# Three weight buffers in place of two for the expert stage, and gate and up rows in runs of 2 KB

## The chip, the cores and the metric

The kernel runs on one core of one Trainium2 chip. Its engines are PE (the matmul engine, TensorE), DVE (VectorE), ACT (ScalarE), POOL (GpSimd) and SP (SyncE, which here only issues DMAs). The metric is the time of one execution on the device, in microseconds (us); lower is better. Everything computed is float32, or float32 split into a high and a low part.

## The reference

Two layers of a decoder trunk are computed for 512 tokens of width 1024. Only the second half of a layer is touched by the change:

```python
def hierarchical_moe(xn, w_rg, b_rg, w_re, b_re, w_g, w_u, w_d):
    t = xn.reshape(-1, d)
    ...                                   # top group of 4, then top 2 of its 4 experts
    gates = jnp.sum(jax.nn.one_hot(gid, N_EXPERTS) * w_e[..., None], axis=1)
    y = jnp.zeros_like(t)
    for e in range(N_EXPERTS):            # 16 experts
        hid = jax.nn.silu(t @ w_g[e]) * (t @ w_u[e])   # 1024 -> 256, twice
        y = y + gates[:, e:e + 1] * (hid @ w_d[e])     # 256 -> 1024
    return y

for l in range(DEPTH):                    # 2 layers
    ...                                   # three kinds of attention, gates, w_out
    x = x + jnp.sum(gates * proj, axis=2) @ w_out[l]
    x = x + hierarchical_moe(rms_norm(x, norm_ffn[l]), ...)
```

The weights of one expert are three matrices of 1 MiB each: gate and up of 1024x256, down of 256x1024.

## The kernel before

Each layer first runs a long chain of projections and attention, in which PE is fed by pieces of `w_in`, `w_branch` and `w_out` (256 KB each, tile `raw`). The last group is `w_out`. As its tiles are finished, DVE adds them to `x_rows` (the residual), POOL multiplies the sum by the gain of the norm into `rows` (`grow_rows`, 8 instructions of 128x512 for each layer, before `row_scale(1)` for all but the last), and SP stores `rows` to `xn_dram` in four DMAs of 512 KB (L1455, semaphore `xn_out`).

Then the router chooses experts: PE turns the left and right halves of `x_rows`, multiplies by the router's weights, and a chain of short DVE instructions (`route`, L1157 on) makes the table of rows for each expert. It waits for `row_scale(1)` by `scale_ready`. The last of the chain is `tab_i` (L1221, semaphore `r_addr`); while it runs, PE repeats dummy transposes (`keep_warm`, L595).

The expert stage takes the 16 experts in a fixed order (`ORDER`), one after the other, each with at most 128 tokens. For one expert e:

- POOL gathers its rows from `xn_dram` into `xg` (L836, two buffers), PE transposes them (`turn_chunk`, 8 transposes, L702), ACT and DVE split them into a high and a low part (`rows_hi`, `rows_lo`).
- The weights come in six pairs of 128x1024: roles 0 to 3 are gate and up (each pair holds two of the 8 blocks of 128 input rows), roles 4 and 5 are down. For each pair ACT writes the high part (`pair_hi`, L665) and DVE the low part (`pair_lo`, L671) into a ring of five places (`xT` and one in `wh`/`wl`). PE multiplies each split pair in three passes (`passes`, L599 to L601), so 24 matmuls for gate and up, and 12 for down.
- ACT and DVE form the hidden rows, PE turns them, and ACT copies the two halves of the result out of PSUM with the gate (L1018, L1024). POOL scatters them with an addition into the output (L842).

PE computes gate and up of expert e+1 while it is at step e, then down of e. ACT's instructions stand in program order: the copy L1018 of one half of the result, then `pair_hi` of the next pair, and so on.

The raw weights land in two buffers, each of six pairs: buffer 0 in `bqkv`, buffer 1 in `q_c` (gate and up) and `head_odd` (down). Expert e uses buffer e mod 2. SP issues all these DMAs. Experts 0 and 1 are loaded behind the last pieces of `w_out` (L1447). Then SP stores `rows`, loads the next layer's first pieces, and enters `experts_sp` (L847). Its step 1 waits for the first gather to land (`xg_in[0]`), and then issues gate and up of expert 2, each pair once DVE has read that place for expert 0; then it stores `x_rows` to the output; and then for each step gate and up of e+1 and down of e, each behind a wait for `pair_lo_ready`. One gate or up DMA (`load_gate_up`, L675) moves 256 KB. In memory a row of these matrices has 256 floats, so the block of rows `(k p)` gives each partition two runs of 1 KB. A down DMA moves 512 KB in runs of 2 KB.

At the end of layer 0 the last scatter must land, and then `x_rows` is read back from the output. `rows` and `x_rows` are not used between the store of `x_rows` and the next layer.

## Time and profile before

| | us |
|---|---|
| median of 3 runs | 1498.8 |
| lowest and highest run | 1497.61 and 1499.75 |
| the profiled execution's own time | 1496.16 |
| its span, from first to last instruction | 1494.3 |
| PE busy | 1442.4 |
| DVE busy | 893.3 |
| ACT busy | 854.4 |
| POOL busy | 405.1 |

The span is what the trace covers; the 1.86 us between it and the execution's own time lie outside it. Times in the rows are us from the start of the span, unless ns is written. A busy time of PE holds overlapped matmuls, so what counts for PE is the distance between starts. In rows of stretches a DMA share of 1.00 says that the core's 16 DMA engines were busy all the time. The expert stages run from about 580 to 745 us (layer 0) and from about 1322 us to the end (layer 1).

### The profile page before, as it was taken

To read this page: it belongs to the slowest core of one execution; us is meant where nothing else is said; L and a number is where in the kernel's file an instruction comes from. 1 tells how busy PE (TensorE), PEld (TensorE's weight loads), DVE (VectorE), ACT (ScalarE), POOL (GpSimd) and SP (SyncE) were. 2 spreads that over 40 slices of the span, in tenths; PEclk is the share of its full clock that TensorE was granted. 3 is DMA by queue.
4 is the path that set the end of the run, shared out by engine and by line. 5 is a ranking of instruction groups with operands and counts; after the bars stand their busy time and mean duration, and the time that the engine had idled before them with its cause. 6 is when DMAs were issued, how large, how long until landed. Compare 5 with 4: busy or idle time off the path is not lost.

```text
span 1494.3 us, 22177 instructions
## 1 busy us (share of the span) xinstructions
PE 1442.4 (97%) x7844; PEld 1142.2 (76%) x7844; DVE 893.3 (60%) x1742; ACT 854.4 (57%) x1588; POOL 405.1 (27%) x547
## 2 busy tenths in 40 slices
PE   8999999999999999999899999999999999999996
PEld 7787777777777887777677877777777788877775
DVE  4456655634554447989735566556345544489986
ACT  5456546655443335888734565466554434368886
POOL 5314227620000024242215043285200000242421
PEclk9999999999999999999999999999999999999998
DMA  7622222222233368999965222222222323769996
GB/s 196 135 66 69 58 71 64 58 64 64 64 98 97 114 213 272 355 348 350 248 151 121 72 64 64 62 64 60 64 64 64 120 85 111 248 241 348 347 354 196
DMA packets 156054, 220.55 MB, mean 148 GB/s; under 512 B 24851, under 2 KB 94163, under 8 KB 155940
## 3 DMA queue, kind: packets, MB, share of 16 engines
q1 hardware_dynamic: 143604, 194.82, 41.4%
q0 software_dynamic: 11328, 21.60, 7.0%
q10 hardware_dynamic: 1008, 2.69, 0.5%
q8 instruction: 63, 1.03, 0.3%
q14 instruction: 51, 0.42, 0.1%
HBM read 210.51 MB, written 25.49 MB: 158 GB/s over the span
## 4 chain that ended last, share of the span: by engine, by line
PE 81%; DVE 7%; ACT 5%; issue 3%; DMA 3%; POOL 0%; DVEq 0%; POOLq 0%; ACTq 0%; SPq 0%
PE bank L599 21%; PE bank L601 20%; PE bank L600 20%; PE bank L1650 4%; PE bank L1634 3%; PE bank L1623 3%; PE bank L1625 2%; DMA raw<-in_w_in_dram 2%; PE bank L702 2%; DVE xT L671 2%; ACT xT L665 1%; PE bank L1683 1%; PE bank L1686 1%; DVE wl L529 1%; DVE prob L2011 1%
## 5 line engine op out<-in xcount | busy, mean ns | idle before, releaser
L599 PE MATMUL bank<-wh,xT 128*128 128x512 f32 (+1 forms) x960 | 392.8, 409 | 9.1 <-DVE wl L529 5.9
L601 PE MATMUL bank<-wh,xT 128*128 128x512 f32 (+1 forms) x960 | 373.2, 389 | 0.0
L600 PE MATMUL bank<-wl,xT 128*128 128x512 f32 (+1 forms) x960 | 372.5, 388 | 0.0
L522 ACT ACTIVATE wh<-raw,gcol 128x512 fp32r<-128x512 f32 (+1 forms) x208 | 148.5, 715 | 250.7 <-PE bank L601 229.8
L529 DVE SCALAR_TENSOR_TENSOR wl<-raw,gcol,wh 128x512 fp32r<-128x512 f32 (+1 forms) x208 | 161.4, 780 | 156.4 <-ACT wh L522 151.6
L599 PEld LDWEIGHTS bank<-wh,xT 128*128 128x128 f32 x960 | 180.4, 188 | 67.8 <-issue 21.1
L601 PEld LDWEIGHTS bank<-wh,xT 128*128 128x128 f32 x960 | 180.2, 188 | 36.9
L600 PEld LDWEIGHTS bank<-wl,xT 128*128 128x128 f32 x960 | 180.8, 188 | 32.1 <-issue 1.4
L1801 ACT ACTIVATE prob<-prob,nmax 128x128 f32<-128x128 f32 (+2 forms) x192 | 106.7, 557 | 99.8 <-DVE nmax L2011 99.3
L2335 POOL TENSOR_TENSOR rows<-x_rows,ac 128x512 f32<-128x512 f32 x16 | 22.2, 1402 | 477.0 <-DVE x_rows L2078 477.0
L2011 DVE CUSTOM_DVE_ANT_0 prob<-bank,mask 128x128 f32<-128x128 f32 (+3 forms) x128 | 57.4, 487 | 138.8 <-PE bank L1625 78.1
L529 DVE SCALAR_TENSOR_TENSOR wl<-raw,wh 128x512 fp32r<-128x512 f32 (+1 forms) x92 | 64.2, 701 | 102.9 <-ACT wh L522 100.0
L522 ACT ACTIVATE wh<-raw 128x512 fp32r<-128x512 f32 (+1 forms) x92 | 57.2, 621 | 109.4 <-PE bank L601 109.3
L599 PE MATMUL bank<-wh,oT 128*128 128x512 f32 (+1 forms) x276 | 112.2, 406 | 3.7 <-issue 1.7
L601 PE MATMUL bank<-wh,oT 128*128 128x512 f32 (+1 forms) x276 | 106.3, 385 | 0.0
L600 PE MATMUL bank<-wl,oT 128*128 128x512 f32 (+1 forms) x276 | 106.0, 384 | 0.0
L671 DVE TENSOR_TENSOR xT<-bqkv,xT 128x1024 fp32r<-128x1024 f32 x76 | 91.2, 1219 | 10.6 <-ACT xT L665 10.3
L599 PE MATMUL bank<-xT,oT 128*128 128x512 f32 x204 | 85.5, 419 | 6.0 <-DVE xT L671 4.4
L842 POOL DMA_INDIRECT out_dram<-ac,tab_i x32 | 53.1, 1658 | 109.9 <-ACT ac L1024 96.5
L665 ACT ACTIVATE xT<-bqkv 128x1024 fp32r<-128x1024 f32 x76 | 78.7, 1057 | 2.9 <-DMA bqkv<-in_w_expert_down_dram 2.1
L601 PE MATMUL bank<-xT,oT 128*128 128x512 f32 x204 | 80.3, 393 | 0.0
L600 PE MATMUL bank<-xT,oT 128*128 128x512 f32 x204 | 79.9, 392 | 0.0
(321 smaller groups left out, 2668.4 us busy)
## 6 DMA issues: line engine op xcount, KB each, us to landing
raw<-in_w_in_dram SPq DMA_DIRECT2D x190, 256.0 KB, 2.7
bqkv<-in_w_expert_gate_dram SPq DMA_DIRECT2D x64, 256.0 KB
bqkv<-in_w_expert_up_dram SPq DMA_DIRECT2D x64, 256.0 KB
bqkv<-in_w_expert_down_dram SPq DMA_DIRECT2D x32, 512.0 KB
q_c<-in_w_expert_gate_dram SPq DMA_DIRECT2D x64, 256.0 KB
q_c<-in_w_expert_up_dram SPq DMA_DIRECT2D x64, 256.0 KB
head_odd<-in_w_expert_down_dram SPq DMA_DIRECT2D x32, 512.0 KB
raw<-in_w_branch_dram SPq DMA_DIRECT2D x48, 256.0 KB, 2.6
```

The source lines that it names most:

```text
L522: nc.scalar.activation(wh[:, i % HL, 0:width], raw[:, i % RAW, 0:width], ACT.Copy, scale=piece_gain(i))\
L529: nc.vector.scalar_tensor_tensor(out=wl[:, i % HL, 0:width], in0=raw[:, i % RAW, 0:width], scalar=piece_gain(i), in1=wh[:, i % HL, 0:width ...
L599: nc.tensor.matmul(out, lhs[0], rhs[0], start=start, stop=False)
L600: nc.tensor.matmul(out, lhs[0], rhs[1], start=False, stop=False)
L601: return nc.tensor.matmul(out, lhs[1], rhs[0], start=False, stop=stop)
L665: nc.scalar.activation(pair_half(pair_ring(e, j, par), 0), pair, ACT.Copy).then_inc(pair_hi_ready, 1)
L671: nc.vector.tensor_tensor(pair_half(pair_ring(e, j, par), 1), pair, pair_half(pair_ring(e, j, par), 0).bitcast(F32), ALU.subtract).then_in ...
L842: nc.gpsimd.indirect_dma_start(out=out_rows, out_offset=bass.IndirectOffsetOnAxis(ap=index, axis=0), in_=src, in_offset=None, bounds_check ...
L1623: mm = pe.matmul(out, q[r, c, qs], k[r, c, 0:w], start=(b == 0), stop=(b == 0 or col + w == 512))
L1650: mm = pe.matmul(o_bank[h * HD:(h + 1) * HD, block * P:(block + 1) * P], val[:, kt, vc:vc + HD], probT[:, h, col + kt * P:col + (kt + 1) * P],
L1801: act.activation(prob[:, h, col:col + w], prob[:, h, col:col + w], ACT.Exp, scale=-1.0, bias=nmax[:, m:m + 1], accum_out=den[:, m:m + 1]). ...
L2011: nc.vector.tensor_tensor_reduce(prob[:, h, col:col + w], sc_bank[h][:, col:col + w], add, -SOFT[b], 3.0e38, ALU.add, ALU.min, nmax[:, m:m ...
```

## The change

A third buffer is added (`NB = 3`), so that expert e uses buffer e mod 3. The new one has gate and up in `rows` and down in `x_rows`. Since `rows` is free once it has been stored to `xn_dram`, and `x_rows` once it has been stored to the output, SP's list at the start of the expert stage is written anew: wait for `xn_out`, issue gate and up of expert 2 with no further wait, wait for the first gather, store `x_rows`, issue gate and up of expert 3, wait for `x_stored`, issue down of expert 2. From then on gate and up of x+1 are issued ahead of down of x, for x from 3 on.

Second, gate and up are read as `(p k)` in place of `(k p)`: partition p takes the 8 rows 8p to 8p+7, which lie side by side, so that two of them are one run of 2 KB, and the next partition's run starts 8 KB further on. For the product to stay the same, the columns of the normed rows are permuted in the same way: `grow_rows` on POOL now reads its inputs in order and writes each group of 8 elements with a step of 128 elements (512 bytes). And in a pair the two gate blocks now stand ahead of the two up blocks, so that PE's moving operand of 512 columns is two runs of 256 with 256 others between them.

```diff
--- before.py
+++ after.py
@@ -39,6 +39,7 @@
 NCH = 23
 OVER_PLACED, OVER_LISTED, OVER_SLOTS = 37, 43, 4
 RAW, HL = 4, 3
+NB = 3
 BIAS_LEN = SEQ + P
 
 
@@ -310,8 +311,10 @@
         raw_slots = [bqkv.rearrange("p (j k c) -> p j k c", j=6, k=2),
                      q_c.rearrange("p h s -> p (h s)").rearrange("p (j k c) -> p j k c", j=4, k=2),
                      head_odd.rearrange("p (j k) c -> p j k c", j=2)]
+        third = [rows.rearrange("p j (k c) -> p j k c", k=2), x_rows.rearrange("p j (k c) -> p j k c", k=2)]
         pair_raw = [[raw_slots[0][:, j] for j in range(6)],
-                    [raw_slots[1][:, j] for j in range(4)] + [raw_slots[2][:, j] for j in range(2)]]
+                    [raw_slots[1][:, j] for j in range(4)] + [raw_slots[2][:, j] for j in range(2)],
+                    [third[0][:, j] for j in range(4)] + [third[1][:, j] for j in range(2)]]
         pair_w = xT.rearrange("p a k s -> p (a k s)").rearrange("p (r h k c) -> p r h k c", r=4, h=2, k=2)
         xgT_all = oT0.rearrange("p a k s -> p (a k s)").rearrange("p (b h k s) -> p b h k s", b=2, h=2, k=KD)
         xgT = [xgT_all[:, 0], xgT_all[:, 1]]
...
@@ -636,9 +640,8 @@
         def pair_place(e, j, par, half):
 
             role = pair_role(e, j)
-            if role < 4:
-                return pair_raw[1 - par][role], pair_in[1 - par][role], 32 * (half + par + 1)
-            return pair_raw[par][role], pair_in[par][role], 16 * (half + 1)
+            x = e + 1 if role < 4 else e
+            return pair_raw[x % NB][role], pair_in[x % NB][role], (32 if role < 4 else 16) * (x // NB + 1)
 
         def pair_multiplied(eng, e, j):
 
@@ -675,18 +678,25 @@
         def load_gate_up(sp, expert, j, par, s_):
 
             for half, w in ((0, "w_expert_gate"), (1, "w_expert_up")):
-                src = at(t[w].rearrange("l e (k p) f -> (l e) p k f", p=P), expert)
-                sp.dma_start(pair_raw[par][j][:, :, half * FF:(half + 1) * FF], src[:, 2 * j:2 * j + 2, :]).then_inc(s_, 16)
+                src = at(t[w].rearrange("l e (p k) f -> (l e) p (k f)", p=P), expert)
+                dst = pair_raw[par][j].rearrange("p k c -> p (k c)")
+                sp.dma_start(dst[:, 2 * half * FF:2 * (half + 1) * FF], src[:, 2 * j * FF:2 * (j + 1) * FF])\
+                    .then_inc(s_, 16)
 
         def load_down(sp, expert, c, par, s_):
             src = at(t["w_expert_down"].rearrange("l e (k p) d -> (l e) p k d", p=P), expert)
             sp.dma_start(pair_raw[par][4 + c], src[:, :, 512 * c:512 * (c + 1)]).then_inc(s_, 16)
 
+        def gate_up_half(r_, a):
+
+            return pair_half(r_, a).rearrange("p k c -> p (k c)").rearrange("p (h k f) -> p k h f", h=2, k=2)
+
         def gate_up(out, x_, r_, j):
 
+            out = out.rearrange("p (h f) -> p h f", h=2)
             for k in range(2):
                 kt = 2 * j + k
-                mm = passes(out, (x_[:, 0, kt], x_[:, 1, kt]), (pair_half(r_, 0)[:, k], pair_half(r_, 1)[:, k]),
+                mm = passes(out, (x_[:, 0, kt], x_[:, 1, kt]), (gate_up_half(r_, 0)[:, k], gate_up_half(r_, 1)[:, k]),
                             kt == 0, kt == KD - 1)
             return mm
 
@@ -849,23 +859,30 @@
 
                 sp.wait_ge(pair_lo_ready, of(pair_lo_ready, value))
 
-            def step(e, par, half):
-
-                if e == 1:
-                    sp.wait_ge(xg_in[0], of(xg_in[0], 16))
-                if not is_const(e, 0) and not is_const(e, NE - 1):
-                    for j in range(4):
-                        passed(j + 1 if is_const(e, 1) else pair_no(e - 2, j) + 1)
-                        load_gate_up(sp, layer * NE + ORDER[e + 1], j, 1 - par, pair_in[1 - par][j])
-                if e == 1:
-                    for n in range(NT):
-                        sp.dma_start(out_tiles[n], x_rows[:, n, :]).then_inc(x_stored, 16)
-                if not is_const(e, 0) and not is_const(e, 1):
-                    for c in range(2):
-                        passed(pair_no(e - 2, 4 + c) + 1)
-                        load_down(sp, layer * NE + ORDER[e], c, par, pair_in[par][4 + c])
-
-            expert_steps(step)
+            def next_gate_up(x):
+                for j in range(4):
+                    passed(pair_no(x - NB - 1, j) + 1)
+                    load_gate_up(sp, layer * NE + ORDER[x], j, x % NB, pair_in[x % NB][j])
+
+            def next_down(x):
+                for c in range(2):
+                    if x >= NB:
+                        passed(pair_no(x - NB, 4 + c) + 1)
+                    load_down(sp, layer * NE + ORDER[x], c, x % NB, pair_in[x % NB][4 + c])
+
+            sp.wait_ge(xn_out, of(xn_out, 16 * NT))
+            for j in range(4):
+                load_gate_up(sp, layer * NE + ORDER[NB - 1], j, NB - 1, pair_in[NB - 1][j])
+            sp.wait_ge(xg_in[0], of(xg_in[0], 16))
+            for n in range(NT):
+                sp.dma_start(out_tiles[n], x_rows[:, n, :]).then_inc(x_stored, 16)
+            next_gate_up(NB)
+            sp.wait_ge(x_stored, 16 * NT * (layer + 1))
+            next_down(NB - 1)
+            for x in range(NB, NE):
+                if x + 1 < NE:
+                    next_gate_up(x + 1)
+                next_down(x)
             if layer + 1 < DEPTH:
                 for q in range(N_GAINS):
                     load_gain(sp, layer + 1, q)
@@ -2332,7 +2349,9 @@
                 def grow_rows(half, n):
                     cs = slice(512 * half, 512 * (half + 1))
                     sums_read(pool, GID["out", half], n)
-                    nc.gpsimd.tensor_tensor(rows[:, n, cs], x_rows[:, n, cs], grow[:, cs], ALU.mult)\
+                    spread = rows[:, n, :].rearrange("q (k p) -> q p k", k=KD)[:, P // 2 * half:P // 2 * (half + 1), :]
+                    nc.gpsimd.tensor_tensor(spread, x_rows[:, n, cs].rearrange("q (p k) -> q p k", k=KD),
+                                            grow[:, cs].rearrange("q (p k) -> q p k", k=KD), ALU.mult)\
                         .then_inc(rows_grown, 1)
 
                 row_scale(0)
```

SP's list at the start of the first expert stage, from the store of `rows` on. The names are tiles and tensors; `pair_lo_ready` counts the pairs that DVE has split, `xg_in0` the first gather, `xn_out` the stores of `rows`, `x_stored` those of `x_rows`. Before:

```order
L1455 DMA xn_dram<-rows 128x1024 [waits rows_grown] x4
L1398 DMA gcol<-in_norm_mix_dram 128x8x1
L477 DMA raw<-in_w_in_dram 128x512 [waits lo_ready] x4
L679 DMA bqkv<-in_w_expert_gate_dram 128x2x256 [waits pair_lo_ready,xg_in0]
...
L679 DMA bqkv<-in_w_expert_up_dram 128x2x256
L862 DMA out_dram<-x_rows 128x1024 x4
L679 DMA q_c<-in_w_expert_gate_dram 128x2x256 [waits pair_lo_ready]
...
L679 DMA q_c<-in_w_expert_up_dram 128x2x256
L683 DMA bqkv<-in_w_expert_down_dram 128x2x512 [waits pair_lo_ready] x2
L679 DMA bqkv<-in_w_expert_gate_dram 128x2x256 [waits pair_lo_ready]
```

And of the changed kernel the same place:

```order
L1472 DMA xn_dram<-rows 128x1024 [waits rows_grown] x4
L1415 DMA gcol<-in_norm_mix_dram 128x8x1
L481 DMA raw<-in_w_in_dram 128x512 [waits lo_ready] x4
L683 DMA rows<-in_w_expert_gate_dram 128x512 [waits xn_out]
...
L683 DMA rows<-in_w_expert_up_dram 128x512
L878 DMA out_dram<-x_rows 128x1024 [waits xg_in0]
L878 DMA out_dram<-x_rows 128x1024 x3
L683 DMA bqkv<-in_w_expert_gate_dram 128x512 [waits pair_lo_ready]
...
L683 DMA bqkv<-in_w_expert_up_dram 128x512
L688 DMA x_rows<-in_w_expert_down_dram 128x2x512 [waits x_stored]
L688 DMA x_rows<-in_w_expert_down_dram 128x2x512
L683 DMA q_c<-in_w_expert_gate_dram 128x512 [waits pair_lo_ready]
L683 DMA q_c<-in_w_expert_up_dram 128x512
```

Gate and up of expert 2 have moved from behind the gather to ahead of it, the store of `x_rows` now waits for the gather itself, gate and up of expert 3 stand where those of expert 2 were, and down of expert 2 has a wait of its own for `x_stored`.

On POOL, the instructions between the last products with `w_out` and the router keep their order, and the ones that write `rows` get another form (the names are tiles; `acc_read` counts the additions of DVE). Before:

```order
L2335 TENSOR_TENSOR rows<-x_rows,ac 128x512 [waits acc_read] x6
L2316 TENSOR_TENSOR ssx<-ssx,ssh 128x4 [waits sum_ready]
L2317 TENSOR_SCALAR ssx<-ssx 128x4 [waits pool_own]
L2318 TENSOR_TENSOR rsx<-ssx,pw 128x4 [waits pool_own]
L2335 TENSOR_TENSOR rows<-x_rows,ac 128x512 [waits acc_read]
```

And of the changed kernel the same five rows:

```order
L2353 TENSOR_TENSOR rows<-x_rows,ac 128x64x8 [waits acc_read] x6
L2333 TENSOR_TENSOR ssx<-ssx,ssh 128x4 [waits sum_ready]
L2334 TENSOR_SCALAR ssx<-ssx 128x4 [waits pool_own]
L2335 TENSOR_TENSOR rsx<-ssx,pw 128x4 [waits pool_own]
L2353 TENSOR_TENSOR rows<-x_rows,ac 128x64x8 [waits acc_read]
```

Nothing moved here: each of the eight writes to `rows` is now 64 groups of 8 elements. PE's list has no difference, and those of ACT and DVE only in the tile that a pair is read from.

## Rows read from the trace of the kernel before

**Rows 1.** Chain that ended last, experts of layer 0: start us, us, what
```profile
628.94 1.06 ACT xT L665
630.02 1.24 DVE xT L671
631.30 0.50 PE bank L599
```

**Rows 2.** Stretches between PE's `turn_chunk`s: busy us by engine, PEclk, DMA share, GB/s
```profile
606.28:616.17 9.89, 9.67 (x48) 7.60 (x47) 8.92 (x11) 8.75 (x12) 2.65 (x2) 1.00 1.08 355
715.02:725.15 10.13, 9.59 (x48) 7.64 (x47) 9.29 (x11) 9.19 (x13) 1.56 (x1) 1.00 1.07 336
1446.49:1456.71 10.22, 9.61 (x48) 7.68 (x47) 9.27 (x10) 8.49 (x13) 3.36 (x2) 1.00 1.07 346
1456.71:1467.45 10.74, 9.60 (x47) 7.68 (x46) 9.55 (x12) 9.63 (x14) 2.53 (x1) 1.00 1.05 345
...
725.15:741.36 16.21, 15.86 (x72) 11.82 (x70) 14.50 (x17) 14.41 (x21) 3.18 (x2) 1.00 0.80 209
1467.45:1483.86 16.41, 16.11 (x73) 11.97 (x71) 13.01 (x15) 13.25 (x19) 3.12 (x2) 1.00 0.61 189
```

**Rows 3.** Timeline of ACT, start us, us, instruction, [idle before, releaser]
```profile
1456.24 1.06 ACT L665 ACTIVATE xT<-bqkv 128x1024 fp32r<-128x1024 f32 x1 [0.85 <-DMA bqkv<-in_w_expert_down_dram]
```

**Rows 4.** Chain that ended last, layer 1, the last experts
```profile
1460.49 1.15 issue
```

**Rows 5.** DMA from 606 to 616 us: queue, packets, MB, engines' share
```profile
q1 hardware_dynamic: 2580, 3.01, 87.2%
```

**Rows 6.** DMA from 554 to 557.5 us, then from 559.5 to 563 us
```profile
DMA packets 1278, 1.24 MB, mean 353 GB/s; under 512 B 71, under 2 KB 1278, under 8 KB 1278
DMA packets 577, 1.41 MB, mean 401 GB/s; under 512 B 42, under 2 KB 42, under 8 KB 577
```

**Rows 7.** DMA, 1303 to 1343 us in 40 slices of 1 us
```profile
GB/s 391 418 395 381 365 74 12 0 0 311 213 0 0 0 0 16 0 57 127 242 136 324 325 276 337 255 338 427 414 414 430 414 393 366 390 379 377 347 347 374
```

**Rows 8.** Timelines of SP, POOL and PE's weight loads at layer 1's first gather
```profile
1302.02 9.74 SPq L1455 DMA_DIRECT2D xn_dram<-rows  x4
1318.68 1.29 POOL L836 DMA_INDIRECT ac<-xn_dram,tab_i  x1 [5.52 <-DVE tab_i L1221]
1322.07 0.85 PEld L702 LDWEIGHTS bank<-ident,ac 128*128 128x128 f32 x8 [0.33 <-DMA ac<-xn_dram,tab_i]
```

**Rows 9.** The same place in layer 0: SP's timeline, and the chain that ended last
```profile
579.42 0.39 SPq L679 DMA_DIRECT2D bqkv<-in_w_expert_gate_dram  x1
574.64 6.09 PE bank L595 x40
```

**Rows 10.** Timelines of POOL and DVE ahead of the router's chain, layer 0
```profile
557.77 1.30 POOL L2335 TENSOR_TENSOR rows<-x_rows,ac 128x512 f32<-128x512 f32 x1 [15.25 <-DVE x_rows L2078]
565.67 0.20 POOL L2316 TENSOR_TENSOR ssx<-ssx,ssh 128x4 f32<-128x4 f32 x1 [2.86 <-ACT gate_t L1744]
566.24 1.01 POOL L2318 TENSOR_TENSOR rsx<-ssx,pw 128x4 f32<-128x4 f32 x1
568.65 0.24 DVE L1174 TENSOR_TENSOR prob<-prob,rsx 128x80 f32<-128x80 f32 x1
```

**Rows 11.** Groups of POOL by form: count, busy us, mean ns, idle before
```profile
L2307 POOL TENSOR_TENSOR rope_t<-rows,sinT 128x64 f32<-128x64 f32 x8 | 2.6, 321 | 0.0
L2316 POOL TENSOR_TENSOR ssx<-ssx,ssh 128x4 f32<-128x4 f32 x2 | 0.4, 201 | 5.7 <-ACT gate_t L1744 5.7
```

**Rows 12.** Timeline of PE: starts of 128-column and 512-column matmuls
```profile
556.81 0.22 PE L1495 MATMUL bank<-oT,wrs 128*40 128x128 f32 x1
...
557.76 0.45 PE L599 MATMUL bank<-wh,xT 128*128 128x512 f32 x1
...
558.52 0.39 PE L599 MATMUL bank<-wh,xT 128*128 128x512 f32 x1
...
560.56 0.60 PE L1482 MATMUL bank<-ident,x_rows 128*128 128x128 f32 x4
```

More of the change, by code:

```diff
@@ L354, in build @@
         RAW_SEMS = [sem(f"raw_in{i}") for i in range(RAW)]
-        pair_in = [[sem(f"pair_in{b}_{j}") for j in range(6)] for b in range(2)]
+        pair_in = [[sem(f"pair_in{b}_{j}") for j in range(6)] for b in range(NB)]
         xg_in = [sem(f"xg_in{b}") for b in range(2)]
@@ L410, in build @@
             PER_LAYER[f"y_read{b}"] = NE
+        for b in range(NB):
             for j in range(6):
-                PER_LAYER[f"pair_in{b}_{j}"] = (32 if j < 4 else 16) * NE // 2
+                PER_LAYER[f"pair_in{b}_{j}"] = (32 if j < 4 else 16) * len(range(b, NE, NB))
         for n in range(NT):
```

## The prediction, on record before the changed kernel was run

> **What bounds the kernel now.** I started with the engines' busy times in the table: PE is busy for 1442 of 1494.3 us, so only what lets PE start earlier counts. I then read the chain of waits that ended last in the expert stage. One expert takes a round of 9.89 us. The reader is to see in [rows 1] what interrupts PE there: ACT copies a result and then splits a pair (1.06 us), DVE makes the low part (1.24 us), and only then PE goes on. No DMA stands in this round, and it repeats with the same length.
>
> Third, I cut the stage into stretches from one `turn_chunk` to the next [rows 2]. In layer 0 the first stretch after start-up is 9.89 us, and the ten behind it are 9.86 to 9.90. The last ones aren't: 10.13 in layer 0, 10.22 and 10.74 in layer 1. All have a DMA share above 1.0 at about 350 GB/s. ACT's timeline says what differs at the end: in the long stretches it waits for weights, once for 0.85 us [rows 3], and PE's gap grows to 1.15 us, for which the chain shows only "issue" [rows 4].
>
> The DMA rows explain why this comes late. From 606 to 616 us the queue of the weights moved 3.01 MB [rows 5]. One expert needs 3 MiB = 3.146 MB in 9.885 us, that is 3.18 MB in 10 us. So the stream falls behind by 0.17 MB in 10 us, or 0.56 us with each expert. Two buffers hide this for about 12 experts (12 x 0.56 = 6.7 us of slack), and the last ones pay. DMA thus bounds the last two or three experts of a layer, while ACT, DVE and PE bound the other thirteen.
>
> **What the third buffer gives.** In layer 1 the stores of `rows` are issued by 1311.76 [rows 8], and their traffic has ended by 1314 (the first 0 after the slices of 311 and 213 GB/s [rows 7]). The DMA engines then stand nearly idle until the loads of expert 2 go out behind the gather, at 1322, and fill them from 1323 on. In layer 0 these loads went out at 579.42 [rows 9], and with the same order of work ahead of them they will go out at about 572. So the stream starts some 7.5 us earlier in each layer, and the third buffer, which is one expert deep, lets it keep that lead. Missing is 0.56 x 13 = 7.3 us, of which 6.7 are already hidden. The lead covers the rest ten times.
>
> **What the 2 KB runs give.** With packets of 1 KB alone the engines moved 353 GB/s while fully busy, with packets of 2 KB and 4 KB 401 GB/s [rows 6]. Gate and up are two thirds of the bytes. An estimate from these rows: the weights' time falls by 2/3 x 12% = 8%, more than the 5.3% that are missing (0.17 of 3.18 MB). Each half of the change alone would remove the shortage. Where the other has already removed it, the second is worth nothing more.
>
> **The sum, against the profiled execution's 1496.16 us.**
> - The long stretches return to 9.885: 10.13 - 9.885 + 10.22 - 9.885 + 10.74 - 9.885 = 1.4 us [rows 2]. This is the whole gain in the middle: -1.4.
> - The two last stretches, 16.21 and 16.41 us [rows 2], contain small waits for weights too. They differ by 0.2, which I take as one that can go; bounds 0 and 1.0 for both. I take -0.3.
> - The first gather. In layer 1 PE already waits 0.33 us for it [rows 8], so any delay is paid in full. Its transfer begins when POOL's instruction ends, at 1319.97. The new loads are issued from 1314.1 on, 8 of 0.47 us, and start to flow about 1 us later, as in rows 7; 2.1 MB at 401 GB/s are 5.2 us, so they end at about 1320.3. In layer 0 they end at about 578 by the same steps, the gather landed at 579.42, and PE was busy with dummy transposes until 580.73 [rows 9], so 1.3 us are free. Bounds 0 and +2.0, for both layers together; I take +0.3.
> - PE's moving operand is now two runs. No row shows such a matmul. From 16 matmuls of 128 columns in 0.95 us and 9 of 512 in 2.04 us [rows 12] a column costs 0.436 ns, and an instruction 3.6 ns besides. If the jump costs as much as an instruction of its own, 768 matmuls (24 x 16 x 2) pay 2.8 us; if nothing, 0. A jump isn't an instruction, and all rows near it are unbroken operands. I take 0.
> - POOL's scattered writes: eight a layer. They cost nothing up to a point. Three of them run from 557.77 on, and then `row_scale` starts at 565.67, released by ACT [rows 10]. Its last instruction ends at 567.25, and DVE reads the result at 568.65. So `row_scale` may start 1.4 us later, at 567.1, and each write may take (567.1 - 557.77) / 3 = 3.1 us in place of 1.3. For the length itself, the nearest rows: a POOL instruction on groups of 16 needs 321 ns for 64 elements, one of 4 elements 201 ns, which is 2.0 ns an element [rows 11], like the unbroken 1.3 us for 512 (2.1 ns an element). I take no change; upper bound, as no row has such a step, three times, 3.9 us. That would delay the router by 3 x 0.8 = 2.4 us in each layer.
> - SP waits for `x_stored` ahead of down of expert 2. Queued behind it are gate and up of expert 4. The stores go out behind the gather, at about 580 in layer 0, and ACT reads down of expert 2 nearly three rounds of 9.89 us later. Hidden, 0.
> - ACT and DVE read other tiles in the same order: 0. At the layer's end nothing changes, as the last scatter hangs on PE's last matmul.
>
> Sum: -1.4 - 0.3 + 0.3 = -1.4 us, 1494.8 for the profiled execution. The three runs' median is 1498.8, 2.6 us above it; against that I predict 1497.4.
>
> **Two rules of the Trainium skill.** Rows 11 show no price for groups of 16. The Trainium skill's page "GPSIMD Engine Reference", section 7 (Performance pitfalls for Q7 kernels), says that reading SBUF with a step above 8 bytes costs about 2.9 cycles an element in place of 1.9, half as much again. It speaks of reads; here the writes have the step of 512 bytes. By it a write of `rows` takes some 1.9 us, which is below the 3.1 us, so the sum would stay. No run here shows such a step yet. For the gather, "DMA: Bandwidth & Descriptors", section "Queues, rings and completion order", says that a DMA engine takes turns between its queues packet by packet. By that the gather shares the engines with what is left of the loads, and is not behind them: the +0.3 above; behind them it would be up to 1 us in layer 1.
>
> **The rivals.**
> - *The timed executions stall more than the profiled one* (30%). They are 2.6 us longer. A stream slower by 1% is enough: 0.1 us an expert, times 13 experts and 2 layers, is 2.6 us. It fits that the shortage is a small difference of large numbers; against it, any other cause would fit as well. The change would then return this too: 1498.8 - 1.4 - 2.6 = 1494.8.
> - *The gain goes elsewhere* (7%). The long stretches stay, as ACT's waits for weights only cover another wait, or the gather takes it back: 1498.8 plus 0.5 = 1499.3.
> - *The jump in PE's operand costs like an instruction* (5%): -1.4 + 2.8 = +1.4, 1500.2.
> - *POOL's writes take three times as long* (5%): +4.8 - 1.4 = +3.4, 1502.2. It decides from 3.1 us a write on.
> - *The wide rows slow the stream down*, the one that ends on the slower side (6%). Neighbouring partitions now read 8 KB apart, in place of 1 KB. Should the stream be slower by a share f, each expert lacks 0.56 + 9.885 f us, and the slack is 6.7 + 7.5 = 14.2 us. With 13 experts it decides from f = 5.4% on; at 10% it costs 13 x 1.55 - 14.2 = 5.9 us a layer, so 11.9 - 1.4 = +10.5, 1509.3. Against it, down's rows lie 4 KB apart with runs of 2 KB, and such packets are in the 401 GB/s of rows 6.
>
> **How the numbers follow.** The forecast, 1497.4, has 47%, with the five rivals 30, 7, 5, 5 and 6%. What a measurement of this kernel can tell from no change is about 0.2%, or 3.0 us: faster is below 1495.8, slower above 1501.8. Faster: the first rival's 30% and 6% of the forecast's upper bounds of gain, 36%. Slower: the wide rows' 6%, the writes' 5% and 3% of PE's and the gather's upper bounds together, 14%. The rest is 50%. The range reaches down to 1498.8 - 1.4 - 1.0 - 2.6 = 1493.8 (the first rival with the tail's bound), and up to 1501.3: 1497.4 plus 1.7 for the gather's bound and 2.8 for PE's would be 1501.9, and both in full are unlikely. It leaves out the rival of the writes and that of the wide rows.
>
> **What the changed profile would show.** Right: all stretches at 9.88 to 9.90 us, ACT with no wait for weights at the last experts, a DMA share below 1.0 at times in the middle, because SP now waits for buffers; the writes of `rows` below 3.1 us; PE's passes 0.23 us apart; the loads of expert 2 issued before the gather. Wrong: writes of `rows` above 3.1 us with a later L1174; passes farther apart; a wait for the gather of much more than 0.33 us; or rounds that get longer than 9.89 us from the middle on.

## The result, and the profile after

The changed kernel is slower. Its median is 1505.63 us (1501.47 to 1507.25, 8 runs) beside 1499.28 us of the kernel before (1496.99 to 1501.48, 8 runs). The ratio is 1.0037, with a 95% interval of 1.0024 to 1.005. The forecast was 1497.4 with a range up to 1501.3, so the time lies outside it. The profiled execution has a span of 1499.6 us, 5.3 more than before.

What was forecast of the rounds came true. The page shows fewer packets (123286), and the stretches between chunks at the end of each layer [rows 2] are now these. The columns are: length, then busy time of PE, PEld, DVE, ACT, POOL, the granted clock, the DMA share, GB/s.

```profile
718.36:728.24 9.88, 9.63 (x48) 7.61 (x47) 8.89 (x11) 8.75 (x12) 1.56 (x1) 1.00 0.86 244
1453.12:1463.00 9.88, 9.64 (x47) 7.61 (x46) 8.91 (x11) 8.74 (x12) 2.63 (x2) 1.00 1.05 362
1463.00:1472.88 9.88, 9.64 (x47) 7.61 (x46) 8.91 (x11) 8.74 (x12) 2.52 (x1) 1.00 0.65 188
```

No stretch is long any more. In the last one of layer 1 the DMA share is only 0.65, so the weights are there early, and ACT has no wait for a DMA in any of the last rounds (0.85 us once in [rows 3]). GpSimd's scattered writes of the normed rows cost nothing, 1.31 us in place of 1.30 [rows 10] (the columns: count, then shortest, median and longest in ns):

```profile
L2353 POOL TENSOR_TENSOR rows<-x_rows,ac x16: 1280/1314/1785, 537.5 to 1312.9; 128x512 f32<-128x512 f32 x16
```

The time went to the start of each expert stage. The chain of waits (start, length, what) has one row there in each layer. The kernel before has one in layer 1 alone, the first line here; the other two are the changed kernel's:

```profile
1318.68 3.35 DMA ac<-xn_dram,tab_i
...
576.76 7.21 DMA ac<-xn_dram,tab_i
...
1321.41 6.05 DMA ac<-xn_dram,tab_i
```

This is the first gather, from the start of GpSimd's instruction to the landing of the rows. PE's timeline in layer 1 shows what follows from it (start, length, line, what, and in brackets the wait ahead). L599 is the dummy transposes (`keep_warm`), L712 the turning of chunk 0, L603 to L605 the first passes:

```profile
1320.15 4.56 PE L599 MATMUL bank<-ident 128*128 128x128 f32 x40
1327.50 1.09 PE L712 MATMUL bank<-ident,ac 128*128 128x128 f32 x8 [2.80 <-DMA ac<-xn_dram,tab_i]
...
1329.57 0.79 PE L603 MATMUL bank<-xT,oT 128*128 128x512 f32 x1
1330.16 0.63 PE L604 MATMUL bank<-xT,oT 128*128 128x512 f32 x1
1330.59 0.63 PE L605 MATMUL bank<-xT,oT 128*128 128x512 f32 x1
...
1333.65 1.03 PE L712 MATMUL bank<-ident,ac 128*128 128x128 f32 x8
```

PE stands still for 2.8 us. Soon after it starts again, its granted clock (the figure ahead of the last two) falls to 0.50, which is 1.2 of 2.4 GHz. The stretches of 1 us from 1328 on have 0.90, then three times 0.50, of which this is the first:

```profile
1329.00:1330.00 1.00, 0.98 (x4) 0.58 (x3) 1.00 (x2) 0.28 (x1) 0.44 (x2) 0.50 0.99 401
```

Passes then stand 0.43 us apart (1330.16 to 1330.59) in place of 0.23. From chunk 0 to chunk 1 PE needs 6.15 us. Before, and in layer 0, that takes 4.9. In layer 0 PE waits only 1.14 us, because its transposes there ran at the low clock for a part and took 7.39 us in place of 4.56.

The account of the two profiled executions, in us (the tail is the last stretch of a layer, as in [rows 2]):

| | layer 0 | layer 1 |
|---|---|---|
| gather's issue to chunk 0, before | 4.80 | 3.40 |
| the same, after | 7.26 | 6.09 |
| so the start comes later by | 2.46 | 2.69 |
| chunk 0 to chunk 1, after less before | 0.06 | 1.25 |
| chunk 1 to the last chunk, after less before | -0.42 | -1.24 |
| the tail, after less before | 0.33 | -0.05 |

The sum is 5.1, of the span's 5.3. The gain is there (-1.7), the later start costs 5.15, the long interval behind it 1.25. In layer 0 the rows land 3.56 us later than before (7.21 in place of 3.65 us behind the issue); 1.1 us of that are hidden behind the transposes.

### The profile page after: what moved, and what is told of

Read it like the earlier page. It is cut to its first block, busy times and chain, and to the rows that moved or that the text cites. A ratio compares the mean times of both kernels' runs of the same rounds, so it can differ in the third digit from the quotient of the medians.

```text
span 1499.6 us, 22175 instructions
## 1 busy us (share of the span) xinstructions
PE 1445.9 (96%) x7844; PEld 1144.9 (76%) x7844; DVE 892.0 (59%) x1742; ACT 853.7 (57%) x1588; POOL 403.0 (27%) x547
## 2 busy tenths in 40 slices
DMA packets 123286, 220.55 MB, mean 147 GB/s; under 512 B 24851, under 2 KB 28627, under 8 KB 123172
## 3 DMA queue, kind: packets, MB, share of 16 engines
q10 hardware_dynamic: 1008, 2.69, 0.5%
## 4 chain that ended last, share of the span: by engine, by line
PE 79%; DVE 8%; ACT 5%; DMA 4%; issue 4%; POOL 0%; SPq 0%; POOLq 0%; DVEq 0%; ACTq 0%
PE bank L603 21%; PE bank L605 19%; PE bank L604 19%; PE bank L1667 4%; PE bank L1651 3%; PE bank L1640 3%; PE bank L1642 2%; DMA raw<-in_w_in_dram 2%; DVE xT L674 2%; PE bank L712 2%; ACT xT L668 2%; PE bank L1700 1%; DMA ac<-xn_dram,tab_i 1%; PE bank L1703 1%; DVE wl L533 1%
## 5 line engine op out<-in xcount | busy, mean ns | idle before, releaser
L603 PE MATMUL bank<-wh,xT 128*128 128x512 f32 (+1 forms) x960 | 393.0, 409 | 8.9 <-DVE wl L533 5.7
L605 PE MATMUL bank<-wh,xT 128*128 128x512 f32 (+1 forms) x960 | 373.2, 389 | 0.0
L603 PEld LDWEIGHTS bank<-wh,xT 128*128 128x128 f32 x960 | 180.6, 188 | 67.1 <-issue 21.1
L605 PEld LDWEIGHTS bank<-wh,xT 128*128 128x128 f32 x960 | 180.3, 188 | 36.9
L603 PE MATMUL bank<-wh,oT 128*128 128x512 f32 (+1 forms) x276 | 112.0, 406 | 2.3 <-DVE wl L674 1.4
L605 PE MATMUL bank<-wh,oT 128*128 128x512 f32 (+1 forms) x276 | 106.2, 385 | 0.0
L603 PE MATMUL bank<-xT,oT 128*128 128x512 f32 x204 | 86.1, 422 | 5.8 <-DVE xT L674 5.4
L605 PE MATMUL bank<-xT,oT 128*128 128x512 f32 x204 | 80.6, 395 | 0.0
L674 DVE TENSOR_TENSOR xT<-bqkv,xT 128x1024 fp32r<-128x1024 f32 x58 | 70.0, 1219 | 8.8 <-ACT xT L668 8.8
L846 POOL DMA_INDIRECT ac<-xn_dram,tab_i x32 | 34.2, 1070 | 134.2 <-PE bank L712 120.8
```

The costliest lines, as they stand in the source:

```text
L603: nc.tensor.matmul(out, lhs[0], rhs[0], start=start, stop=False)
L605: return nc.tensor.matmul(out, lhs[1], rhs[0], start=False, stop=stop)
L674: nc.vector.tensor_tensor(pair_half(pair_ring(e, j, par), 1), pair, pair_half(pair_ring(e, j, par), 0).bitcast(F32), ALU.subtract).then_in ...
```

## Why the gather is late

SyncE's queue in layer 0 (start, length of the group of issues, line, what):

```profile
570.35 2.49 SPq L481 DMA_DIRECT2D raw<-in_w_in_dram  x4
572.88 0.43 SPq L683 DMA_DIRECT2D rows<-in_w_expert_gate_dram  x1
...
577.88 0.33 SPq L683 DMA_DIRECT2D rows<-in_w_expert_up_dram  x1
```

The eight new loads stand where they should, but right ahead of them go four loads of the next layer's input weights, 1 MB. In layer 1 these aren't there, and the new loads are alone (first at 1316.84, last at 1320.27). There the traffic, in stretches of 1 us, is (columns as above):

```profile
1318.00:1319.00 1.00, 0.43 (x4) 0.19 (x2) 0.93 (x6) 0.34 (x1) 0.00 (x0) 1.00 0.72 246
1319.00:1320.00 1.00, 0.43 (x11) 0.34 (x12) 0.87 (x6) 0.00 (x0) 0.00 (x0) 1.00 0.60 195
1320.00:1321.00 1.00, 1.00 (x16) 1.00 (x17) 0.67 (x2) 0.00 (x0) 0.00 (x0) 1.00 0.85 238
...
1323.00:1324.00 1.00, 1.00 (x11) 1.00 (x10) 0.93 (x6) 0.06 (x1) 1.00 (x1) 1.00 1.10 408
```

The next rows of that table go 387, 375, 205 and 21 GB/s. The loads' last packets move at about 1326.5, and behind that only the gathers' are left. Split by queue (packets, MB, share of the 16 engines; q0 is that of the gathers, the second of which is issued at 1323.00, and q1 that of the loads) the two stretches 1324 to 1325 and 1325 to 1326 are:

```profile
q1 hardware_dynamic: 203, 0.37, 96.3%
q0 software_dynamic: 5, 0.02, 5.0%
...
q0 software_dynamic: 136, 0.25, 70.8%
q1 hardware_dynamic: 74, 0.12, 34.2%
```

GpSimd's instruction had ended at 1322.71. In the kernel before the same instruction ends at 1319.97, with its rows landed 2.1 us later. There its first packets move within 1.1 us of the instruction's end. Here 2.3 us pass, until 1325, with 5 packets of the gather (beside 203 of the loads in the last of them), and the rows come when the loads are through. What keeps the gather's packets back in that time, the engines or the making of them, no view shows.

## The experiments

The theory (A) was: traffic of the early loads holds the first gather back, that is on PE's path in both layers, and it is the whole loss. The rival (B): the third buffer's place, its waits, or the 2 KB rows cost the time. All ratios are to the kernel before on the same chip, with 95% intervals. "Gather" is from issue to landing by the chain, or, where PE didn't wait for it and there is no such row, to the start of chunk 0 (marked <).

| run | median, before | ratio | gather, layer 0 / 1 |
|---|---|---|---|
| changed kernel | 1505.63, 1499.28 | 1.0037 (1.0024 to 1.005) | 7.21 / 6.05 |
| changed kernel again | 1506.57, 1498.49 | 1.0049 (1.0036 to 1.0062) | 7.28 / 6.02 |
| e1 none of the 8 loads ahead | 1496.31, 1497.43 | 0.9992 (0.998 to 1.0005) | < 4.48 / < 4.81 |
| e4 four ahead | 1500.53, 1497.43 | 1.0017 (1.0006 to 1.0029) | 4.70 / 3.33 |
| e2 eight ahead, 1 KB | 1502.9, 1497.43 | 1.0035 (1.0022 to 1.0047) | 7.21 / 6.09 |
| e3 two buffers, 2 KB | 1496.2, 1497.43 | 0.9995 (0.9982 to 1.0008) | 3.98 / < 3.33 |
| e5 old kernel, 8 unused loads | 1505.42, 1499.44 | 1.0039 (1.0023 to 1.0055) | 7.33 / 5.32 |
| e6 52 transposes | 1504.48, 1499.44 | 1.0037 (1.0023 to 1.005) | 8.19 / < 6.23 |
| e7 none ahead, 28 transposes | 1497.31, 1499.44 | 0.9991 (0.9978 to 1.0005) | < 3.59 / 4.42 |
| e8 loads at the gather's issue | 1503.43, 1499.44 | 1.0027 (1.0015 to 1.0039) | 6.58 / 6.09 |
| e9b six loads by tile | 1506.15, 1498.49 | 1.0044 (1.003 to 1.0058) | 5.58 / 3.80 |

**e1_loads_behind_gather.**

```
-            for j in range(4):
-                load_gate_up(... third buffer ...)
             sp.wait_ge(xg_in[0], of(xg_in[0], 16))
+            for j in range(4):
+                load_gate_up(... third buffer ...)
```

> The changed kernel with the eight gate and up loads of expert 2 issued behind the landing of the first gather in place of ahead of it; three buffers and 2 KB rows stay. Theory A (the 2 MiB of early loads hold the first gather back, on the path): the gather is back to about 3.5 us from issue to landing in both layers (7.2 and 6.1 in the changed kernel), the second interval of layer 1 is back under 5 us, and the time falls by 4 to 6 us against the changed kernel, to 1497 to 1500, within 2 us of the kernel before. Rival B (the loss lies in the third buffer or the 2 KB rows themselves: the stores of x, the GpSimd writes, slower passes): the time stays at 1504 to 1507. Rival C (the loads must go somewhere: they hold back the next gathers or the x stores instead): between, 1501 to 1504.

Measured: 0.9992, and all rounds are 9.84 to 9.93 us. The trace has the landing 3.6 and 3.4 us behind the gather's issue; chunk 0 starts 0.9 and 1.4 us after it, because the dummy transposes ran partly at the low clock and took 5.92 and 6.23 us. A's gather and its interval (4.86 us) came; the time, 1496.31, is 0.7 us below its range. At the later place the loads cost nothing that the interval would show, so rivals B and C fall.

**e2_three_buffers_1KB**: the load, the passes' operand and the write of `rows` as in the kernel before, three buffers and early loads as in the changed one.

> The changed kernel with the gate and up weights in runs of 1 KB again (the loads' old form, the old layout of the gains, the old operand of the passes); three buffers and the early loads stay. Theory A: the same 2 MiB now come in twice as many packets, so the first gather is held back as long or a little longer, 6 to 8 us from issue to landing; time 1505 to 1509, as slow as the changed kernel or slower. Rival B2 (the 2 KB packets hold the gather back, each turn in the round of the queues being longer): the gather lands 1 to 2 us sooner than in the changed kernel in each layer and the time is 1501 to 1503.

Measured: 1.0035, 7.21 and 6.09 us: the same gather to a few hundredths, with packets of half the size. The 2 KB rows have no part in the late gather. No part of the loss by the passes' two-run operand is seen either: the two ratios agree within their 0.0013, and the passes of the changed kernel stand 0.23 us apart at the high clock. The time, 1502.9, is below A's range of 1505 to 1509 and inside that of B2, but the kernel before is faster on this chip too (1497.43), so the ratio counts; B2's sooner gather didn't come. The rounds were all 9.9 us, so the early start alone also removes the shortage.

**e3_two_buffers_2KB**: the same three edits in the other direction, on the kernel before.

> The kernel before, with the gate and up weights in runs of 2 KB and all that belongs to it; two buffers, no early loads. Theory A: the first gather is as before (3.4 to 3.7 us), and shorter transfers take part of the shortage of weights away: 1496.5 to 1499.5, up to 2.5 us under the kernel before. Rival B (2 KB rows cost time in the passes or on GpSimd): 1500 to 1504.

Measured: 0.9995 (1496.2, 0.3 us below A's range), gather 3.98 us in layer 0, all rounds 9.9 us. The 2 KB rows alone remove the shortage; the third buffer isn't needed.

**e4_half_ahead**: `range(2)` ahead of the wait, `range(2, 4)` behind it.

> The changed kernel with only the first four of the eight gate and up loads of expert 2 ahead of the first gather (1 MiB), the other four behind its landing. Theory A: the delay goes by the bytes still queued when the gather's rows are asked for, so about half of it or less: the gather at 4 to 5.5 us from issue, the time 1499 to 1503, between the run with none ahead and the changed kernel. Rival D (the delay is one of order, any load ahead costs it whole): 1504 to 1507.

Measured: 1.0017, about half of the loss. In layer 1 the four loads were over soon after 1318 (27 GB/s from 1318 to 1319), and the gather took 3.33 us, as if alone; in layer 0, behind the 1 MB of input weights, 4.70. So it isn't order that costs, but what is still under way. The profile doesn't account for the median, though: its execution took 1493.33 us, and chunk 0 starts 4.74 and 3.38 us behind the issue, no later than in the kernel before (4.80 and 3.40). There the transposes of layer 0 took 6.24 us, here, at the high clock, 4.57, and so the gather of 4.70 us made PE wait 1.45 us and still lost nothing.

**e5_old_plus_loads**, on the kernel before (`unused` is waited for at the end of the stage):

```
+            sp.wait_ge(xn_out, of(xn_out, 16 * NT))
+            for j in range(4):
+                for half, w in ((0, "w_expert_gate"), (1, "w_expert_up")):
...
+                    sp.dma_start(dst[...], src[...]).then_inc(unused, 16)
```

> The kernel before (two buffers, 1 KB rows) with eight loads of 256 KB added ahead of the first gather, at the place where the changed kernel has its loads of expert 2; they go into the normed rows' memory and nothing reads them. Theory A (traffic that is queued ahead of the gather is the whole loss): the gather takes 7 to 7.5 us from issue to landing in layer 0 and 6 to 6.5 in layer 1, and the time is 5 to 8 us above the kernel before, 1502 to 1506 on a chip where that one has 1497.4. Rival B (the third buffer's place or its other waits are needed for the loss): under 1500.

Measured: 1.0039, the loss of the changed kernel, with two buffers and 1 KB rows. Its gather takes 7.33 and 5.32 us; layer 1 is below what A expected. So the traffic beside the gather is enough for a loss of this size. This kernel keeps its shortage of weights (the last four rounds of layer 1 are 10.36, 10.21, 10.63 and 10.65 us), so it lacks the changed kernel's gain; the 0.001 that this makes is less than the intervals can tell. That nothing else in the change adds to the loss is shown, within its interval, by e1.

**e6_warm_52**: `keep_warm(h_bank[1], 52)` in place of 40.

> The changed kernel with 52 in place of 40 dummy transposes on TensorE ahead of the first chunk. Theory A with the clock as a second part (TensorE stands idle for 2.8 to 4 us behind its 40 transposes, the granted clock falls to the lower level and the next passes stand 0.43 us apart in place of 0.23): the drop goes away, the interval from chunk 0 to chunk 1 is 4.9 us in both layers, and 0.5 to 1.5 us come back against the changed kernel, with the gather as late as there. Rival (the clock falls for another reason): an interval of 5.8 us or more stays in one layer. If the clock is low ahead of the transposes, 12 more cost up to 1 us.

Measured: 1.0037, nothing came back, and this run doesn't price the clock. The gather took 8.19 us in layer 0 of its profile, PE still waited 2.40 us, and the interval was 5.92. In layer 1 the transposes outlasted the gather, and the interval was 4.94. Over the profiles with a wait of PE for the gather the picture is the same. Behind nine waits of 0.42 to 1.85 us (the longest in e8, layer 0) chunk 0 to chunk 1 took 4.91 to 4.98 us. Behind waits of 2.40 (e6), 2.60 and 2.80 (changed kernel), 3.79 and 4.09 (e9b), 3.97 (e2) and 4.08 us (e5) it took 5.79 to 6.15, once 6.95 (e9b). So behind the longer waits the interval is 0.8 us or more longer. That the late gather brings this about is argued from these profiles; no run sets the wait alone. The clock is also low during the transposes in many profiles, e1's and e7's among them, where no gather is late.

**e7_behind_warm_28**: e1 with 28 transposes.

> The changed kernel with the loads of expert 2 behind the first gather (as in e1_loads_behind_gather) and 28 in place of 40 dummy transposes. In e1's layer 0 the transposes ran partly at the lower clock, took 5.92 us and ended later than the gather landed. With 28 chunk 0 starts when the gather lands: up to 1 us less than e1 in each layer whose clock is low there, nothing where it is high; 1494.5 to 1496.5 beside 1497.4 of the kernel before. Rival (fewer transposes let the clock fall): 1497 to 1500.

Measured: 0.9991 beside e1's 0.9992. No gain that can be seen, and no loss.

**e8_loads_after_ask**: SyncE waits for a semaphore that GpSimd raises behind its first gather instruction, and then issues the eight loads.

> The changed kernel with the eight loads of expert 2 issued when GpSimd's first gather instruction has ended (not when its rows have landed): the gather is asked for first, the loads share the engines with it. Theory A in the form 'what is queued ahead counts': the gather takes 3.4 to 4.2 us from issue to landing, the time is that of e1, 1496 to 1498. Rival D ('the engines take turns, so any load beside the gather slows it'): 4.5 to 6 us from issue to landing in layer 1 and a time of 1499 to 1503.

Measured: 1.0027, 6.58 and 6.09 us. This form of A, "only what is queued ahead counts", is wrong. Rival D is nearer, with a gather and a time (1503.43) just above its ranges. The semaphore comes when the instruction starts, not when it ends: first load 1326.25, gather 1326.38. So the loads flow first here too. Split by queue, 1330 to 1331:

```profile
q1 hardware_dynamic: 59, 0.10, 44.0%
q0 software_dynamic: 65, 0.10, 33.2%
```

Here packets of both queues move in the same microsecond, and together only 0.2 MB. The gather lands at 1332.47, and the loads still flow (289 GB/s from 1332 to 1333, and more behind that), so it isn't last of all.

**e9b_loads_by_tile**: in the loop that stores the normed rows, ahead of tile 3:

```
+                    if n == NT - 1:
+                        sp.wait_ge(xn_out, of(xn_out, 16 * (NT - 1)))
+                        for j in range(NT - 1):
+                            load_gate_up(... third buffer ...)
```

> The changed kernel with six of the eight loads of expert 2 (the pairs whose memory the normed rows of tiles 0 to 2 leave first) issued ahead of the store of tile 3, when the first three stores have landed: about 2 us after the third store, 4 to 5 us sooner than in the changed kernel. The last two loads stay behind the fourth store. Theory A (the gather is held back by traffic that is still open in its own time, so loads that are over by then cost nothing): layer 1 has no other traffic, its gather takes 3.4 to 4.5 us from issue to landing (6.1 in the changed kernel); layer 0 has 1 MB of the next layer's input weights behind the stores too, its gather takes 4.5 to 6 us. Time 1 to 4 us under the changed kernel. Rival E (the 1.5 MB now hold back the store of tile 3, and the gather is asked for later): GpSimd's first gather instruction comes 1 us or more later against its table's last step, and nothing is won.

Measured: 1.0044, 1506.15 us beside 1506.57 of the changed kernel on the same chip, so A's gain of 1 to 4 us didn't come. Theory A was right on the gather, rival E on the time. The loads were over when the gather came, and it took 3.80 us in layer 1. But the store of tile 3, issued at 1325.77, landed 6.9 us later, and GpSimd waits for it:

```profile
1333.52 1.20 POOL L846 DMA_INDIRECT ac<-xn_dram,tab_i  x1 [9.07 <-DMA xn_dram<-rows]
```

The wait moved from the gather to the store that feeds it. At none of the three places tried for six or all eight of them ahead of the gather's landing (here, e8 and the changed kernel) were the loads free.

**after_once_more**, the changed kernel unedited.

> The changed kernel once more, beside e9b_loads_by_tile on the same chip: 1.0037 of the kernel before, within 0.0013. If the delay of the gather is the whole loss, the profile shows it again: 7 to 8.2 us from issue to landing in layer 0, 6.0 to 6.3 in layer 1, and an interval of 5.8 us or more from chunk 0 to chunk 1 only where TensorE stood idle for over 2.4 us.

Measured: 1.0049, gather 7.28 and 6.02, the long interval (6.11) this time in layer 0 behind a wait of 2.60 us. So in each of the two profiles one layer has the long interval and the other hasn't.

**e10b_behind_1KB**: e1 with e2's 1 KB rows.

> Three buffers with the loads of expert 2 behind the first gather, as in e1_loads_behind_gather, but gate and up in runs of 1 KB as in the kernel before. My working says that the 2 KB rows alone remove the shortage of weights and that the third buffer helps by its lead: here the lead is gone (the first loads go out as late as before, only one buffer deeper), and the stream is as slow as before, 0.56 us short an expert. So the last rounds of a layer stay long: 10.1 to 10.7 us, and the time is within 1 us of the kernel before. Rival: the depth of three buffers alone evens the stream out, all rounds are 9.88 us, and it is 1.5 us faster, as e1.

Measured: 1500.46 us beside 1499.45, 1.0009 (0.9997 to 1.002). The shortage is back, with three buffers:

```profile
704.72:715.24 10.52, 9.62 (x48) 7.68 (x47) 8.00 (x9) 8.28 (x12) 3.67 (x2) 1.00 1.08 349
715.24:729.70 14.46, 11.43 (x48) 8.82 (x46) 11.58 (x14) 10.68 (x14) 1.56 (x1) 0.88 1.03 330
```

Layer 1 has one of 10.48 us.

One round, 14.46 us, is far outside what was expected. A load of up weights landed 10.91 us after its issue, ACT waited 1.89 us for it and PE in turn 2.73 us, and then the granted clock fell to 0.50 and passes stood 0.43 us apart. This execution (1503.71 us) is among the slowest of its kernel (up to 1504.07), so the median doesn't stand for it. A third buffer without a lead, filled by a stream that is slower than its use, doesn't remove the shortage.

**e11b_two_buffers_2KB_again** and **e12b_behind_again**, the kernels of e3 and e1.

> The kernel of e3_two_buffers_2KB once more, for the size of its gain. By the long stretches of the kernel before (1.4 us in all) and the first result (0.9995 within 0.0013): a ratio of 0.9985 to 0.9997; all rounds 9.88 us.

> The kernel of e1_loads_behind_gather once more, for the size of its gain: a ratio of 0.9985 to 0.9997 of the kernel before, no difference from e11b that the runs can tell; the gather lands 3.3 to 4.4 us after its issue in both layers.

Measured: 0.9985 (0.9974 to 0.9997) and 0.9992 (0.9979 to 1.0004), medians 1497.38 and 1497.77 beside 1499.45. The gather part of the second was right: 3.6 and 3.3 us by the trace's landing. In layer 0 the transposes outlasted it, and chunk 0 starts 4.65 us behind the issue. The two results of e3 have a mean of 0.9990, those of e1 of 0.9992; the 1.4 us that the long stretches are worth would be 0.9991. The gain is of the forecast size, but only one of the four intervals excludes 1. No run tells e1 and e3 apart; e3 is the simpler one, with neither a third buffer nor a wait for `x_stored` on SyncE.

## Why the prediction was wrong, step by step

- **What bounds the last experts**: right. A stream 5.3% too slow was the cause of the long stretches. Either half of the change removes them (e2, e3), and the second is worth nothing more.
- **Long stretches -1.4**: right, -1.66 from chunk 1 to the last chunk in both layers. **Tails -0.3**: they came out at +0.3, outside the bounds (0 and -1.0). Why isn't known.
- **GpSimd's writes, PE's two-run operand, `x_stored`**: 0 each. For the writes and the operand the rows show it; the wait for `x_stored` has no row of its own, but e1 has it too and loses nothing. The Trainium skill's "GPSIMD Engine Reference", section 7 (Performance pitfalls for Q7 kernels), let one expect half as much again for a step above 8 bytes when reading. The trace doesn't show that for writes: 1.31 us with a step of 512 bytes, 1.30 without.
- **The first gather +0.3, bounds 0 and +2.0**: this is the step that failed. It measured 2.46 + 2.69 = 5.15 us. The sign of being wrong that the prediction named, a wait for the gather of much more than 0.33 us, is what came: 1.14 and 2.80 us. Three things in it were wrong. First, the mass: for layer 0 it said "by the same steps" and left out the four loads of the next layer's input weights (1 MB), which go out just ahead in the kernel before too. The traffic there ended at about 583.5, not 578. Second, the rate: 2.1 MB at 401 GB/s. That is the rate of a stream in full flow, and in part that of stores with 4 KB packets. In layer 1 the new loads began with 195 to 246 GB/s and were over at about 1326.5, where the forecast's 1320.3, moved by the 2.7 us by which this execution ran later, is 1323.0. The forecast's own [rows 7] had a slow start of this kind: from 1323 to 1330, behind the gather, 136 to 338 GB/s. Third, the bounds: they priced what is left of the loads when the gather starts. A wait that is already 0.33 us long [rows 8] has no slack, and the upper bound should have been worked out with the rates of a stream's start, such as those of rows 7, and in layer 0 with 3.1 MB.
- **The clock**: the forecast took a wait of PE as its own length. In layer 1 the interval behind it is 1.25 us longer, at a granted clock of 0.50.
- **The rule on turns**: the Trainium skill's "DMA: Bandwidth & Descriptors", section "Queues, rings and completion order", has the engines take turns between queues packet by packet. This case's traces neither confirm nor refute that: in the changed kernel's layer 1 one microsecond has 5 packets of the gather beside 203 of the loads, in e8 one has 65 beside 59, but no view shows from when on the gather's packets stood ready. The gather took 6.1 us in both. So the forecast's step from that rule to a small delay ("the +0.3 above") failed, in whatever way the engines share.
- **The rivals**: "the gain goes elsewhere" named the gather taking it back, at 7% and 1499.3. It was this mechanism, with its price far too small: 0.5 us above the kernel before, where 6.35 us were measured between the medians. The three others with a later time (PE's operand, GpSimd's writes, a slow stream of wide rows) didn't occur. The stall of the timed runs that was to come back (30%) didn't show: e1 and e3 gain what the profile says and not 2.6 us more (4.0 us in all would be a ratio of 0.9973, just below all four intervals). The round of 14.46 us in e10b shows what such a stall can look like.

How much of the 6.35 us between the medians is clock can't be told: in each of the two profiles one layer had the long interval, and no run parts it from the wait.

## What to carry to other kernels

Before loads are moved to an earlier, idle-looking place, list everything on the queues there, and then ask which small transfer on the critical path starts while they are still under way. As an upper bound price it as if it came last; in the changed kernel's layer 1 it nearly did, in e8 it landed with loads still flowing, and where the loads were over (e4, layer 1) it lost nothing. If an engine already waits for that transfer, however shortly, every microsecond counts, and TensorE's clock can add to it. Here the stream was 5% too slow, and larger packets cured it without touching the order of work (e3), while a third buffer without a lead did not (e10b); so packets are worth trying first.

## What the runs showed of the hardware

- The same eight loads of 256 KB began more slowly in 2 KB rows than in 1 KB rows: 195 to 246 GB/s in the first three full microseconds of layer 1 in the changed kernel, 329, 277 and 219 in e2, and 263, 298 and 293 in e5. The second profile of the changed kernel has 217, 193 and 139. In full flow it is the other way round [rows 6]. Why is open.
- Forty dummy transposes took 4.56 us at the high clock and up to 7.39 us where the clock was low for a part of them (changed kernel, layer 0). In that layer of the kernel before they, and not the gather, set the start of chunk 0.
- A semaphore raised by GpSimd right behind an indirect DMA came at its start, 1.3 us before the instruction's end (e8, layer 1).
- PE's granted clock was 0.50 behind a wait of 2.73 us in the middle of the stage too (e10b), not only at its start.
